# Low halves one or two units behind the high halves in the attentions of a two-block transformer kernel

## The chip, the core and the metric

The kernel runs on one core of a Trainium2 chip. The metric is device time in microseconds of one execution, as the median of several runs. The profile is of one further execution of the same program.

## The reference

Two transformer parts run one after the other, all in float32, on 512 tokens (the "latent" side) of width 1024; the first part also carries 256 context tokens.

- First part, two layers. A modulated RMS norm, one projection to queries (8 heads of 64), keys and values (2 groups of 64), and two gated inputs. Queries and keys get an RMS norm and a rotary embedding. `s = einsum('bkgqd,bkmd->bkgqm', q, k)`, `p = softmax(s)`, `einsum('bkgqm,bkmd->bkgqd', p, v)`; the latent queries see context and latent keys (768), the context queries (first layer only) the 256 context keys. Beside it a spatial gating block (4 groups). Their results are put together and multiplied by `w_out`; then a squared-ReLU feed-forward.
- Second part, two layers. A gated feed-forward, a mixer, another gated feed-forward. The mixer has 6 MLA heads (96 wide), a pooling branch and 6 "Fox" heads (64 wide, with a cumulated decay added to the scores), both attentions causal over 512 keys.

So there are five attention stretches: context and latent in layer 1, latent in layer 2, and the two mixers.

## The kernel before

**High and low halves.** A matrix product is made in a reduced format: each float32 operand x is split into a high half, ScalarE's copy of x to that format, and a low half, x minus high, which VectorE makes (`low`, L1844 and L1845: a subtraction with two tensor operands). TensorE adds high x high and the cross products (L819 to L821 for the weights' products). Weights are split the same way, by `split` on ScalarE (L1398) and on VectorE (L1779), one chunk of 128 output columns at a time in two buffers. SP's queue loads a chunk when the low half of the chunk two before is made.

**The order.** The code of each engine is one long list written out by hand; engines meet through counting semaphores, and each engine works in order. So an instruction that waits holds up all that stands behind it on its engine.

**An attention** is a loop over units; a unit is one head and 128 queries. Two heads make a pair, and their units alternate, so a pair has 8 units (4 in the context attention). Units: 16 context, 32 latent, 48 mixer. In step u:

- TensorE (`scores`, L1304 and L1305, or L1319 to L1322 in the mixer) makes the scores of unit u in one of 2 slots (4 in the mixer), as soon as the exponential of the unit that had the slot is through. It waits for the low halves of a head's queries (`q_los`) only at the head's first unit, and for those of the keys (`k_los`). Then `turn_p` (L1338) transposes the weights of unit u-3 (u-4 in the mixer), and `values` (L1366) multiplies two units' weights with the values.
- VectorE takes the negated maximum (L2269), in the first part multiplied by the query's scale (L2274), then the reciprocal of the sum of unit u-1 (L2280) and, in the first part, copies the second group of turned weights (L2287).
- ScalarE copies turned weights (L1720), then makes the exponential with its sum (L1730), which waits for VectorE's maximum.
- GpSimd multiplies the weights of a unit by the reciprocal (L2366), and in the mixer sets constant rows for heads to come (L2373 to L2376).

**Work for later that lies between.** At given units ScalarE makes high halves and VectorE the low ones: of the queries of the next pair's heads (`prepares`: units 1 and 3 of a pair, 0 and 2 in the context attention; in the mixer both queries and keys, `prepare2`, and for four Fox heads a third, small piece), of a finished pair's result (`take_out` on ScalarE, `lower_out` on VectorE), of the gated block's results (`gm`: high at odd units from 3, low at the even unit behind), of the pooling branch (high at 6, low at 7), and of the first two weight chunks of the product to come (ScalarE at 2 and 3, VectorE at 3 and 4). Queries' and results' low halves stand at the same unit as the high halves. `lower_k` makes both low halves of the second key group at unit 2, in the context attention of layer 1 and in the latent attention of layer 2.

One load of the modulation weights on SP's queue also waits for the last query low of the context attention.

The loop of VectorE around the change:

Of the kernel before, what the change touches and what calls it, by code (L numbers as in the profile page):

```python
# [23 lines left out]
KD = D // P  # L24
# [77 lines left out]
def build_program(nc, a, out):  # L102
    from contextlib import ExitStack
    ctx = ExitStack()
    with ctx:
# [151 lines left out]
        for l in range(L):  # L257
# [17 lines left out]
            for s in more[::-1]:  # L275
                nq = W[s] // P
                keys = C + T if s == "lat" else C
                U = 8 * nq
# [316 lines left out]
        def prepares(st, u):  # L595

            pair, r = divmod(u, 2 * st.nq)
            at = (1, 3) if st.nq > 2 else (0, 2)
            if r not in at:
                return None  # L600
            hd = 2 * pair + 2 + at.index(r)
            if st.first:
                if hd < st.heads:
                    return st.s, hd
                return ("lat", hd - st.heads) if st.s == "ctx" else None
            return hd if hd < st.heads else None

# [51 lines left out]
        with nc.Block() as block:  # L659
# [1104 lines left out]
            def _(dve):  # L1764
# [97 lines left out]
                def lower_k(qk, kv):  # L1862

                    own = slice(64 * kv, 64 * kv + 64)
                    dve.wait_ge(S["k_his"], qk.at("k_his", 2 * kv + 2))
                    for half in range(2):
                        low(k_lo[kv][64 * half:64 * half + 64, :], k_all[own, :], k_hi[own, kv, :]
                            ).then_inc(S["k_los"], 1)

                for st in stages:  # L1870
# [383 lines left out]
                    elif st.kind == "attention":  # L2254
# [9 lines left out]
                        for u in range(U + lag(st) + 3):  # L2264
# [23 lines left out]
                            if st.first and u >= 4 and u % 2 == 0 and u // 2 - 1 <= len(st.gm):  # L2288

                                s2, g = st.gm[u // 2 - 2]  # L2290
                                dve.wait_ge(S["gm_hi"], st.at("gm_hi", u // 2 - 1))
                                low(HL[s2][:, 4 + g, :], zt(6 + g, s2), HH[s2][:, 4 + g, :]).then_inc(S["gm_lo"], 1)
                            if not st.first and u == 7:
# [3 lines left out]
                            if u < U and prepares(st, u):  # L2297
                                if st.first:
                                    n_prep += 1
                                    prepare(st.at("q_his", n_prep), *prepares(st, u))  # L2300
                                else:
                                    n_prep += 2
                                    prepare2(st, st.at("q_his", n_prep - 1), prepares(st, u))
                            if not st.first and u in (3, 4):
                                split(st.chunk0 + u - 3, u - 3, KD)
                            if st.first and st.last_keys and u == 2:
                                lower_k(st.qk, 1)
                            v = u - lag(st) - 3
# [112 lines left out]
```

## Time and profile before

| | |
|---|---|
| median of 3 runs | 3521.12 us (3520.13 to 3521.68) |
| the profiled execution | 3524.67 us |
| its span in the trace | 3522.9 us |
| busy: TensorE / VectorE / ScalarE / GpSimd | 3410.5 / 1836.8 / 1200.4 / 369.0 us |
| chain that ended last, by engine | PE 87%, DVE 6%, ACT 4%, issue 2%, POOL 1% |
| mean granted TensorE clock | 0.982 |

PE is TensorE's products, PEld its loads of the stationary operand, DVE VectorE, ACT ScalarE, POOL GpSimd. Busy time of an engine is the time in which one of its instructions runs; the ends of matmuls are modelled, so a busy TensorE need not be at its peak. "Chain" is the work followed back from the last instruction, at each step to what released it. PEclk is the clock that TensorE was granted, as a share of 2.4 GHz; it has two levels, 1.0 and 0.5, and other values are means over a stretch. In a timeline row, the bracket gives how long the engine had been idle and what released it.

### The profile page before, as it was taken

How to read it: one execution, taken by the hardware profiler on the slowest of the kernel's cores; microseconds unless marked ns; L12 is line 12 of the kernel's file. 1: busy time of each engine (PE TensorE's matmuls, PEld its weight loads, DVE VectorE, ACT ScalarE, POOL GpSimd, SP SyncE). 2: the span in 40 equal slices, each digit the busy share in tenths (PEclk: the TensorE clock that was granted, in tenths of full speed). 3: DMA queues.
4: the chain of work that ended last, by engine and by line, in shares of the span. 5: the costliest groups of instructions: out<-in, count | busy, mean ns of one | idle time of the engine just before them, and what ended most of it. 6: DMA issues, size and time to landing. Idle time of an engine off the chain costs nothing.

```text
span 3522.9 us, 47185 instructions
## 1 busy us (share of the span) xinstructions
PE 3410.5 (97%) x17172; PEld 2804.5 (80%) x17172; DVE 1836.8 (52%) x2785; ACT 1200.4 (34%) x1886; POOL 369.0 (10%) x415
## 2 busy tenths in 40 slices
PE   9989999999998999999999989999999999899999
PEld 5867888888877788888888667888888886678887
DVE  5766866455357444454345665434543455654343
ACT  4354222122146332333232364323332323643232
POOL 0013200000202200020001132000200011320001
PEclk9989999999999999999999989999999999999999
DMA  6300343333220133333333302333333333023332
GB/s 220 118 29 25 96 137 106 117 130 125 61 72 24 49 95 96 96 95 95 97 99 102 83 25 60 97 99 95 90 101 96 95 96 83 25 61 98 98 95 90
DMA packets 551251, 314.75 MB, mean 89 GB/s; under 512 B 31102, under 2 KB 524888, under 8 KB 551128
## 3 DMA queue, kind: packets, MB, share of 16 engines
q1 hardware_dynamic: 550608, 312.99, 29.9%
q8 instruction: 76, 1.25, 0.1%
q14 instruction: 47, 0.39, 0.0%
q10 hardware_dynamic: 520, 0.13, 0.0%
HBM read 310.98 MB, written 2.10 MB: 89 GB/s over the span
## 4 chain that ended last, share of the span: by engine, by line
PE 87%; DVE 6%; ACT 4%; issue 2%; POOL 1%; DMA 0%; SPq 0%; DVEq 0%; ACTq 0%; POOLq 0%
PE ps L819 26%; PE ps L821 26%; PE ps L820 26%; PE ps L1338 2%; PE ps L1366 1%; DVE nmax L2269 1%; PE ps L974 1%; DVE scr L1956 1%; ACT scr L1730 1%; PE ps L1304 1%; ACT w_hi_sb L1398 1%; DVE hl_lat L1944 0%; PE ps L1138 0%; DVE x_ctx L1784 0%; PE ps L1244 0%
## 5 line engine op out<-in xcount | busy, mean ns | idle before, releaser
L1779 DVE TENSOR_TENSOR w_lo_sb<-w_raw,w_hi_sb 128x1024 fp32r<-128x1024 f32 (+1 forms) x460 | 588.5, 1280 | 1236.3 <-ACT w_hi_sb L1398 1234.7
L1398 ACT ACTIVATE w_hi_sb<-w_raw 128x1024 fp32r<-128x1024 f32 (+1 forms) x460 | 506.3, 1101 | 1382.2 <-PE ps L821 1351.4
L819 PE MATMUL ps<-hh_lat,w_lo_sb 128*128 128x512 f32 x1808 | 720.1, 398 | 6.0 <-DVE w_lo_sb L1779 1.9
L820 PE MATMUL ps<-hl_lat,w_hi_sb 128*128 128x512 f32 x1808 | 706.0, 391 | 0.0
L821 PE MATMUL ps<-hh_lat,w_hi_sb 128*128 128x512 f32 x1808 | 705.6, 390 | 0.0
L819 PEld LDWEIGHTS ps<-hh_lat,w_lo_sb 128*128 128x128 f32 x1808 | 341.2, 189 | 84.6 <-issue 6.7
L820 PEld LDWEIGHTS ps<-hl_lat,w_hi_sb 128*128 128x128 f32 x1808 | 340.9, 189 | 74.9 <-issue 6.3
L821 PEld LDWEIGHTS ps<-hh_lat,w_hi_sb 128*128 128x128 f32 x1808 | 340.6, 188 | 72.2
L819 PE MATMUL ps<-h2h,w_lo_sb 128*128 128x512 f32 x704 | 275.2, 391 | 1.9 <-DVE z L2240 1.5
L820 PE MATMUL ps<-h2l,w_hi_sb 128*128 128x512 f32 x704 | 274.0, 389 | 0.0
L819 PE MATMUL ps<-m2h,w_lo_sb 128*128 128x512 f32 x704 | 273.9, 389 | 0.0
L821 PE MATMUL ps<-h2h,w_hi_sb 128*128 128x512 f32 x704 | 273.9, 389 | 0.0
L821 PE MATMUL ps<-m2h,w_hi_sb 128*128 128x512 f32 x704 | 273.9, 389 | 0.0
L820 PE MATMUL ps<-m2l,w_hi_sb 128*128 128x512 f32 x704 | 273.9, 389 | 0.0
L819 PE MATMUL ps<-m1h_lat,w_lo_sb 128*128 128x512 f32 x512 | 200.4, 391 | 2.7 <-DVE x_ctx L2177 2.7
L820 PE MATMUL ps<-m1l_lat,w_hi_sb 128*128 128x512 f32 x512 | 199.5, 390 | 0.0
L821 PE MATMUL ps<-m1h_lat,w_hi_sb 128*128 128x512 f32 x512 | 199.4, 389 | 0.0
L2334 POOL TENSOR_TENSOR x_ctx<-x_lat 128x512 f32<-128x512 f32 x7 | 7.3, 1042 | 1577.8 <-DVE x_lat L2177 1577.8
L819 PEld LDWEIGHTS ps<-h2h,w_lo_sb 128*128 128x128 f32 x704 | 132.2, 188 | 31.1 <-DVE z L2240 2.3
L2366 POOL TENSOR_SCALAR scr<-scr,rinv 128x768 f32<-128x768 f32 (+4 forms) x120 | 90.3, 753 | 616.1 <-DVE rinv L2280 615.3
L820 PEld LDWEIGHTS ps<-h2l,w_hi_sb 128*128 128x128 f32 x704 | 132.2, 188 | 27.7 <-issue 0.5
L821 PEld LDWEIGHTS ps<-h2h,w_hi_sb 128*128 128x128 f32 x704 | 132.2, 188 | 27.7
(361 smaller groups left out, 5359.7 us busy)
## 6 DMA issues: line engine op xcount, KB each, us to landing
w_raw<-in_ffn_w_gu SPq DMA_DIRECT2D x176, 512.0 KB, 3.8
w_raw<-in_w_ff SPq DMA_DIRECT2D x128, 512.0 KB, 4.0
w_raw<-in_ffn_w_down SPq DMA_DIRECT2D x64, 704.0 KB, 4.5
z<-in_w_mod SPq DMA_DIRECT2D x64, 512.0 KB, 5.1
w_raw<-in_w_in SPq DMA_DIRECT2D x56, 512.0 KB, 3.8
w_raw<-in_w_out SPq DMA_DIRECT2D x32, 512.0 KB, 3.9
scr<-in_w_mod SPq DMA_DIRECT2D x16, 512.0 KB, 5.1
scr<-in_w_mod SPq DMA_DIRECT2D x2, 2048.0 KB, 14.5
```

Source lines behind the costliest of these rows:

```text
L819: nc.tensor.matmul(dst, wl, hi[:, k, 0:n], start=(k == 0), stop=False)
L820: nc.tensor.matmul(dst, wh, lo[:, k, 0:n], start=False, stop=False)
L821: mm = nc.tensor.matmul(dst, wh, hi[:, k, 0:n], start=False, stop=(k == kt - 1))
L974: mm = nc.tensor.matmul(bank(5 + n % 3)[0:2, :], silu_c[:, :, k], mod_slot(n)[:, k, :], start=(k == 0), stop=(k == KD - 1))
L1304: nc.tensor.matmul(dst[:, c0:c1], q, k_hi[:, hd // 4, c0:c1], start=True, stop=False)
L1338: mm = nc.tensor.transpose(bank(4 + i % 2)[:, j * P:(j + 1) * P], p[:, kt * P:(kt + 1) * P], ident)
L1366: mm = nc.tensor.matmul(pair_bank(st, pair)[64 * r:64 * r + 64, qt * P:(qt + 1) * P], val, att_pt(st, v - 1 + r, kt * P, (kt + 1) * P), st ...
L1398: nc.scalar.activation(w_hi_sb[:, slot, 0:width], w_raw[:, slot, 0:width], ACT.Copy).then_inc(S["w_hi"], 1)
L1730: nc.scalar.activation(att_p(st, u, n), s_slot(st, u, n), ACT.Exp, bias=nmax[:, i:i + 1], scale=q_scale(st, u) if st.first else 1.0, accum ...
L1779: nc.vector.tensor_tensor(w_lo_sb[:, slot, 0:width], w_raw[:, slot, 0:width], w_hi_sb[:, slot, 0:width].bitcast(F32), ALU.subtract).then_i ...
L1956: nc.vector.scalar_tensor_tensor(norm_tmp[i % 2][:, 0:W[s]], X[s][:, m, :], st.a_col(s, m), rs_home(st, s), ALU.mult, ALU.mult).then_inc(S ...
L2366: nc.gpsimd.tensor_scalar(pr, pr, rinv[:, i:i + 1], 0.0, ALU.mult, ALU.add).then_inc(S["p_norm"], 1)
```

## The change

The order of VectorE's instructions inside the attention loops changes; no instruction is added, and no other engine's list changes.

- The low halves of queries (and keys in the mixer) come two units behind the high ones in the latent and mixer attentions, one unit behind in the context attention (`low_behind`).
- The low half of a pair's result comes later by as many units.
- The low halves of the gated block's results go from even to odd units, two units behind the high ones.
- In the mixer the pooling low halves go from unit 7 to 8, and the low halves of the two weight chunks from units 3 and 4 to 5 and 6.
- The second key group's two low halves go from unit 2 to units 4 and 6, one each.

```diff
@@ -604,6 +604,10 @@
+
+        def low_behind(st):
+
+            return 2 if st.nq > 2 else 1
@@ -1859,11 +1863,11 @@
-                def lower_k(qk, kv):
+                def lower_k(qk, kv, halves=(0, 1)):

                     own = slice(64 * kv, 64 * kv + 64)
                     dve.wait_ge(S["k_his"], qk.at("k_his", 2 * kv + 2))
-                    for half in range(2):
+                    for half in halves:
                         low(k_lo[kv][64 * half:64 * half + 64, :], k_all[own, :], k_hi[own, kv, :]
                             ).then_inc(S["k_los"], 1)
@@ -2285,27 +2289,28 @@
-                            if st.first and u >= 4 and u % 2 == 0 and u // 2 - 1 <= len(st.gm):
+                            if st.first and u >= 5 and u % 2 and u // 2 - 1 <= len(st.gm):
...
-                            if not st.first and u == 7:
+                            if not st.first and u == 8:
...
-                            if u < U and prepares(st, u):
+                            w = u - low_behind(st)
+                            if 0 <= w < U and prepares(st, w):
                                 if st.first:
                                     n_prep += 1
-                                    prepare(st.at("q_his", n_prep), *prepares(st, u))
+                                    prepare(st.at("q_his", n_prep), *prepares(st, w))
                                 else:
                                     n_prep += 2
-                                    prepare2(st, st.at("q_his", n_prep - 1), prepares(st, u))
-                            if not st.first and u in (3, 4):
-                                split(st.chunk0 + u - 3, u - 3, KD)
-                            if st.first and st.last_keys and u == 2:
-                                lower_k(st.qk, 1)
-                            v = u - lag(st) - 3
+                                    prepare2(st, st.at("q_his", n_prep - 1), prepares(st, w))
+                            if not st.first and u in (5, 6):
+                                split(st.chunk0 + u - 5, u - 5, KD)
+                            if st.first and st.last_keys and u in (4, 6):
+                                lower_k(st.qk, 1, (u // 2 - 2,))
+                            v = u - lag(st) - 3 - low_behind(st)
                             if 0 <= v < U - 1 and pair_ends(st, v):
                                 lower_out(v // (2 * st.nq))
```

## Rows read from the trace of the kernel before

**Rows 1.** Windows; columns: us, PE, PEld, DVE, ACT, POOL busy, PEclk, DMA, GB/s.

```profile
205.00:236.00 31.00, 19.04 (x116) 13.60 (x118) 19.88 (x71) 19.08 (x54) 7.72 (x16) 0.72 0.06 15
236.00:330.00 94.00, 83.32 (x730) 67.90 (x727) 64.26 (x152) 59.86 (x116) 29.11 (x32) 0.95 0.04 13
1076.00:1172.00 96.00, 84.41 (x728) 68.87 (x729) 66.61 (x154) 60.69 (x115) 29.91 (x32) 0.93 0.02 7
2048.00:2138.00 90.00, 77.28 (x571) 62.16 (x570) 53.08 (x134) 62.70 (x179) 38.30 (x66) 0.87 0.05 13
3016.00:3106.00 90.00, 73.23 (x567) 58.30 (x567) 52.77 (x134) 62.70 (x178) 38.28 (x66) 0.92 0.05 13
```

**Rows 2.** Waits, 236 to 330 us: total us, times, longest us.

```profile
ACT scr L1730 <- DVE nmax L2274: 20.3, 22, 2.4
DVE q_hl L1845 <- ACT q_hl L1423: 10.1, 6, 2.1
...
DVE hl_lat L1845 <- ACT hh_lat L1423: 6.7, 4, 3.0
```

**Rows 3.** Timeline, first latent attention: start us, us, engine, operation, idle before.

```profile
248.89 0.69 DVE L1845 TENSOR_TENSOR q_hl<-z,q_hl 64x512 fp32r<-64x512 f32 x1 [2.15 <-ACT q_hl L1423]
```

**Rows 4.** Timeline, first latent attention, two units with TensorE full.

```profile
254.13 1.53 PE L1366 MATMUL ps<-scr 128*64 128x128 f32 x24
...
258.06 0.95 DVE L2269 TENSOR_REDUCE nmax<-ps 128x1 f32<-128x768 f32 x1
...
258.57 1.53 PE L1366 MATMUL ps<-scr 128*64 128x128 f32 x24
...
259.37 0.91 POOL L2366 TENSOR_SCALAR scr<-scr,rinv 128x768 f32<-128x768 f32 x1 [0.55 <-DVE rinv L2280]
259.51 1.30 DVE L1845 TENSOR_TENSOR hl_lat<-z,hh_lat 128x512 fp32r<-128x512 f32 x1
```

**Rows 5.** Windows, latent attentions by eights of exponentials (303.43: seven).

```profile
259.76:282.78 23.02, 19.51 (x178) 15.20 (x174) 17.75 (x40) 15.74 (x33) 7.06 (x9) 1.00 0.01 1
282.78:303.43 20.65, 18.68 (x174) 15.10 (x172) 15.32 (x38) 14.63 (x29) 7.09 (x8) 1.00 0.01 2
303.43:320.19 16.76, 16.00 (x160) 13.50 (x154) 10.91 (x31) 11.48 (x22) 6.38 (x7) 1.00 0.00 1
1082.55:1105.04 22.49, 17.10 (x110) 13.25 (x112) 17.62 (x37) 14.30 (x28) 7.54 (x8) 0.77 0.00 1
```

**Rows 6.** Instructions of L1845, low halves: ns min/median/max, first and last start.

```profile
L1845 DVE TENSOR_TENSOR hl_lat<-ps,hh_lat x20: 691/692/693, 276.8 to 3104.3; 128x512 fp32r<-128x512 f32 x20
```

**Rows 7.** Timeline, second latent attention, VectorE, unit 2.

```profile
1087.37 2.54 DVE L1845 TENSOR_TENSOR k_lo<-scr,k_hi 64x768 fp32r<-64x768 f32 x2
```

**Rows 8.** Windows, context attention: units 0 to 7, units 8 to 14.

```profile
206.64:219.64 13.00, 8.34 (x42) 6.66 (x42) 9.36 (x31) 7.82 (x25) 3.38 (x7) 0.52 0.00 1
219.64:233.56 13.92, 7.76 (x66) 5.27 (x62) 8.79 (x32) 8.33 (x24) 3.38 (x7) 0.97 0.00 1
```

**Rows 9.** Windows, second mixer: units 1 to 4, 17 to 24, 33 to 40.

```profile
3019.06:3028.83 9.77, 5.15 (x27) 4.03 (x26) 6.93 (x16) 6.45 (x17) 2.61 (x4) 0.79 0.07 19
...
3046.92:3062.03 15.11, 11.36 (x93) 8.73 (x92) 9.81 (x24) 11.04 (x33) 9.53 (x16) 1.00 0.00 1
...
3077.12:3089.84 12.72, 10.88 (x92) 8.72 (x92) 7.60 (x22) 9.78 (x30) 5.51 (x10) 1.00 0.00 1
```

**Rows 10.** Timeline, first mixer, a unit that prepares a Fox head.

```profile
2079.17 0.39 ACT L1730 ACTIVATE z<-ps,nmax 128x128 f32<-128x128 f32 x1
...
2079.51 1.84 ACT L1423 ACTIVATE split_x<-z 64x512 fp32r<-64x512 f32 x3
...
2080.18 1.73 DVE L1845 TENSOR_TENSOR split_x<-z,split_x 64x512 fp32r<-64x512 f32 x2 [1.06 <-ACT split_x L1423]
...
2081.93 0.75 DVE L1845 TENSOR_TENSOR split_x<-z,fox_cr 6x512 fp32r<-6x512 f32 x1
...
2083.17 0.47 ACT L1730 ACTIVATE z<-ps,nmax 128x256 f32<-128x256 f32 x1 [1.20 <-DVE nmax L2269]
```

## The prediction

> **What bounds the kernel now.** I read the page first (TensorE busy nearly all the span), then the chain of waits, which puts 87% of the span on TensorE. So only stretches where TensorE runs dry can give time back. The change touches the five attention stretches alone; the windows over them [rows 1] add up to 401.0 us with TensorE busy 337.3. The rest, 31.00 - 19.04 = 12.0 us in the context attention and 10.7, 11.6, 12.7 and 16.8 us in the other four, is 63.7 us and the ceiling of what filling gaps can bring. No engine is full there: VectorE 256.6 us, ScalarE 265.0. The gaps come from order, not load.
>
> The waits of the first latent attention [rows 2] name the order. VectorE stands 10.1 us in six waits for ScalarE's high halves of queries and 6.7 us in four for those of results; ScalarE stands 20.3 us for VectorE's scaled maximum. The timeline of one such unit [rows 3]: VectorE idles 2.15 us until the high half is there and only then makes the low half and goes on to the next maximum. All the while the scores of that unit had been ready: VectorE's queue holds the maximum behind a low half that nobody needs for units to come.
>
> Without such a wait the loop is TensorE's: from one value product to the next [rows 4] it takes 258.57 - 254.13 = 4.44 us for two units, so 17.8 us for eight. The last eight units, which prepare nothing, run close to that: 16.76 us for seven, 0.76 of it idle [rows 5]. The eight units from 259.76 take 23.02 us and the next eight 20.65 [rows 5], with 3.5 and 2.0 us of TensorE idle. That is the cost that the change aims at.
>
> **Part 1: low halves of queries, results and block inputs later, latent attentions.** Nothing is added; the order on VectorE alone changes. Each moved low half finds its high half made a unit or two ago, so the waits of [rows 2] go: 10.1 + 6.7 us of VectorE's time in this stretch, of which TensorE's idle time is the part that reaches the end. Next late is VectorE itself. Its unit costs 259.51 - 258.06 = 1.45 us [rows 4], and a low half of a block input 1.30. A fed eight (four block lows, two query lows at 0.69 [rows 3], one result low at 0.69 [rows 6]) is then 11.6 + 5.2 + 1.4 + 0.7 = 18.9 us, against TensorE's 17.8: VectorE is just the bound where the block inputs are lowered, and not elsewhere (at most 14.9). So the eight of 23.02 falls to about 18.9 but loses no more than the idle 3.5 in TensorE's count; I take 2.9 of it, 1.6 of the 2.0 in the next (block lows in its first half), 0.5 of the last 0.76, and 1.3 in the first eight: 6.3 us. Ends: 3 (one gap in two refilled by the odd units, which now carry two lows) and 9.
>
> The second latent attention has half the block lows, but its first eight take 22.49 us with 5.4 idle [rows 5]. There the two lows of the second key group stand together for 2.54 us [rows 7] at unit 2, ahead of a maximum. In two pieces at units 4 and 6 they are some 1.3 us each when TensorE has scores in stock; the maximum of unit 3 comes these 2.5 us earlier, and the wait for the first query high, of the kind of [rows 3], goes as well. I take 3.3 of the 5.4, and 3.4 of the 6.2 idle elsewhere in that stretch, in all 6.7 us of 11.6. Ends 3 and 11. The keys' deadline is head 4, unit 16 here and unit 8 in the context attention; the pieces are done at 4 and 6, so the wait on them moves only there, by under 1 us.
>
> **Part 2: context attention.** 13.00 us for its first eight units, 13.92 for the next seven [rows 8], the latter at nearly full clock with 6.2 idle. VectorE is busy 8.79 of 13.92. Here lows are one unit behind; the wait for a high half is then about the high itself, beside an exponential. TensorE is no bound in the second half. VectorE's 8.79 and ScalarE's 8.33 busy us are the floor for seven units, 5.1 us below the 13.92; I take 4.0 us of that and 1.0 of the first, where the key lows are only spread and the clock is low (0.52). Sum 5.0; ends 2 and 8.
>
> **Part 3: the two mixer attentions.** 9.77 us for units 1 to 4 with 4.6 idle, then 15.11 us for the eights with Fox heads and 12.72 for the next [rows 9]. A unit that prepares a head [rows 10]: three highs 1.84 us, lows from 2080.18 to 2082.68 (1.73 and 0.75), the next exponential 4.00 us after the last. The same again two units on. So before, each stop is the first high plus the lows, some 3.3 us beyond a plain unit, 6.6 for both heads. Afterwards the first highs stand alone (1.8), the first head's lows lie beside the second head's highs (1.8 more on ScalarE, or 2.5 on VectorE less one exponential), and the second head's lows stand alone (2.5 less the 1 us that ScalarE still has to do): 5.1 to 5.6. That is a gain of only 1 to 1.5 an eight, 1.3 taken; two such eights. The result's low saves about 1 us of VectorE's wait per pair, where TensorE isn't dry for lack of it: 1.0 for the eight of 12.72, 0.3 in the last. The first units lose their wait before the weight split, which moves to units 5 and 6 and there holds a maximum 1.2 us each while TensorE has work: I take 1.5 (first mixer, which has 12.7 us idle to the second's 16.8) and 2.6 us (second) out of idle. Sum 5.4 + 6.5 = 11.9; ends 0 (three lumps as dear as two) and 20.
>
> **Part 4: queues.** The weight loads two chunks on wait for the splits, now some three units later; they are needed after the attention, tens of us away: nothing. The modulation block's load behind the last context query low moves by under one unit, with the whole latent attention as cover: nothing. If that cover were gone each would cost its delay, 1 to 5 us.
>
> **Part 5: the shared access.** What spoke against the old order also shielded it. After its wait a query low met an idle GpSimd and took 0.69 us [rows 3]. A block low that follows the reciprocal at once took 1.30 [rows 4], while GpSimd normalized from 259.37 for 0.91; the same subtraction with one operand in PSUM takes 0.69 [rows 6]. So lows that come right behind the reciprocal may cost 0.6 more, or hold GpSimd's normalization by their own length. For the 6 + 6 query lows of the latent attentions and 20 heads of mixer lows most fall where VectorE has slack. I charge 2 us in all; ends 0 and 37 (see the slower rival). The Trainium skill (SBUF — State Buffer, section "SBUF: two separate sides") states this rule: a VectorE operation with two SBUF inputs and a GpSimd operation that reads SBUF exclude each other for a whole instruction. The trace agrees, 1.30 against 0.69 us.
>
> **Sum.** 6.3 + 6.7 + 5.0 + 11.9 - 2 = 27.9 us. The profiled execution took 3524.67 us (its span is 3522.9), so 3496.8; the median of the runs is 3.55 us below it: 3493.
>
> **The clock.** It is at 1.2 GHz for part of each stretch (granted 0.72 to 0.95 [rows 1]; 0.77 in the first eight of the second latent attention, after 5.4 us of idle in them [rows 5]). Fewer gaps may keep it at 2.4 GHz. Five stretches x (1 - granted) x 2 is about 78 us at the lower level; even a quarter of that regained, at half a us each, is 10 us. It is not in the sum.
>
> **Rivals.**
> - *The lumps stay* (0.22). Lows that lay beside highs now stand alone, and odd units carry block and query lows together. Mixers give 0, the latent attentions 4 each, the context 4: 12 us, 3509. For it: VectorE 18.9 against 17.8 in fed eights, three lumps for two. Against: four scores in stock in the mixers, TensorE well below full there [rows 9].
> - *The clock comes too* (0.11): 27.9 + 10 to 15, 3481 at 10, 3478 and below at the end. For it: the clock rows. Against: entry into each attention is unchanged, and that is where it falls.
> - *No change* (0.03): TensorE's idle time just moves from one unit to another, so that it catches up and starves again; its busy 16.00 of 16.76 [rows 5] shows that it sets the pace where it has work. Within 3 us.
> - *Slower* (0.03): in place of the wait on ScalarE each of some 60 lows (8 + 6 + 6 + 40) excludes GpSimd or is excluded, 0.61 us each on VectorE or on the transposes' path: 37 us lost against 28 gained, 3530. It decides from 0.5 us per low on the path. Against: TensorE takes up a normalized tile units later, and existing block lows pay it in a loop that still keeps TensorE full [rows 4].
> - That the lows aren't released at all cannot be: their waits are on counts that ScalarE reached a unit or more before.
>
> **Numbers.** The forecast, 20 to 36 us gained (3485 to 3501), has 0.61. To hold 8 in 10 the range reaches to the lumps' 3509 and to the clock's 3479. Faster by over 0.2% (7 us, about what a measurement of this kernel can tell from no change): all of forecast, clock and lumps, 0.94; same 0.03; slower 0.03.
>
> **What would show it.** Right: VectorE's waits on ScalarE's high halves near zero in the five stretches (only short ones in the context attention); eights of the latent attentions at 18 to 19 us; mixer eights at about 13.7 instead of 15.1; TensorE idle in the five stretches near 35 us instead of 64; the other stages unchanged. Wrong: new waits of the transposes on GpSimd, ScalarE waiting as long for maxima as before (20.3 us in the first latent attention), low halves of 1.3 us throughout, or scores waiting for low queries or keys.

## The result: faster, by more than the range allowed

| | before | after |
|---|---|---|
| median of the runs taken side by side | 3521.40 us (4 runs, 3520.13 to 3524.96) | 3479.13 us (4 runs, 3476.11 to 3479.71) |
| after / before | | 0.9877 (0.986 to 0.9894) |
| span of the profiled execution | 3522.9 us | 3477.7 us |
| mean granted TensorE clock | 0.982 | 0.985 |

The change takes 42.3 us off the median (27.9 were forecast) and 45.2 off the profiled span. The ratio is the record's, from all the single runs; the medians as they stand give 0.9880. Applied to the median that the prediction started from it gives 0.9877 x 3521.12 = 3477.8 us (3478.9 with 0.9880), just under the lower end of 3479. The sign and the mechanism came as forecast, the size did not.

The page of the changed kernel: busy times, and the chain by engine. VectorE's and ScalarE's work is what it was; GpSimd is busy 18.1 us longer with the same 415 instructions; TensorE's share of the chain rises from 87 to 90%.

```profile
PE 3396.5 (98%) x17172; PEld 2800.6 (81%) x17172; DVE 1838.3 (53%) x2785; ACT 1200.7 (35%) x1886; POOL 387.1 (11%) x415
...
PE 90%; DVE 5%; ACT 3%; issue 1%; POOL 1%; DMA 0%; SPq 0%; DVEq 0%; ACTq 0%; POOLq 0%
```

The windows of [rows 1] in the changed kernel, each over the same work:

```profile
205.00:229.50 24.50, 19.84 (x127) 13.94 (x128) 20.23 (x71) 18.76 (x54) 9.88 (x16) 0.78 0.07 16
229.50:312.80 83.30, 78.79 (x721) 66.25 (x718) 65.33 (x150) 60.26 (x116) 29.18 (x32) 0.97 0.05 16
1058.40:1146.60 88.20, 81.77 (x728) 68.64 (x728) 68.98 (x153) 61.01 (x115) 29.17 (x32) 0.94 0.03 7
2019.40:2102.20 82.80, 75.07 (x571) 61.87 (x570) 52.20 (x134) 62.67 (x179) 46.63 (x66) 0.88 0.05 14
2978.50:3060.50 82.00, 74.27 (x567) 61.29 (x566) 52.28 (x134) 62.74 (x180) 46.65 (x66) 0.88 0.05 14
```

They add up to 360.8 us against 401.0. TensorE is idle in 31.1 us of them (360.8 - 329.7); 35 was forecast from 63.7. But its busy time fell too, from 337.3 to 329.7, for the same products (2712 and 2714 matmuls in the windows). That is what no term of the sum had.

Narrower windows sort it by attention: context with first latent, second latent, first mixer, second mixer. First before, then after:

```profile
206.64:320.19 113.55, 92.06 (x738) 73.00 (x738) 80.02 (x209) 73.96 (x162) 35.02 (x46) 0.89 0.05 15
1082.55:1162.42 79.87, 70.23 (x606) 57.10 (x606) 58.03 (x137) 54.85 (x104) 28.09 (x30) 0.94 0.00 1
2050.93:2130.89 79.96, 69.37 (x509) 55.95 (x508) 50.09 (x127) 59.22 (x171) 36.90 (x64) 0.85 0.05 14
3018.61:3099.35 80.74, 66.09 (x509) 52.78 (x508) 50.10 (x127) 59.42 (x171) 36.89 (x64) 0.92 0.05 14
```

```profile
206.77:302.95 96.18, 87.90 (x739) 71.39 (x739) 80.32 (x208) 73.99 (x162) 37.24 (x46) 0.92 0.06 18
1064.87:1137.01 72.14, 67.41 (x607) 56.81 (x607) 59.86 (x136) 55.37 (x104) 27.35 (x30) 0.95 0.01 1
2022.28:2095.06 72.78, 66.31 (x498) 55.00 (x497) 48.71 (x126) 59.26 (x171) 45.55 (x65) 0.86 0.06 16
2981.47:3054.25 72.78, 66.31 (x498) 55.01 (x497) 48.70 (x126) 59.26 (x172) 45.58 (x65) 0.86 0.06 16
```

| less, in us | forecast | time | TensorE idle | TensorE busy |
|---|---|---|---|---|
| context + first latent | 5.0 + 6.3 = 11.3 | 17.4 | 13.2 | 4.2 |
| second latent | 6.7 | 7.7 | 4.9 | 2.8 |
| first mixer | 5.4 | 7.2 | 4.1 | 3.1 |
| second mixer | 6.5 | 8.0 | 8.2 | -0.2 |
| all four | 29.9 | 40.2 | 30.4 | 9.8 |

The time of a stretch is firmer than its split. These windows run from the first exponential to the last, and the mixers' now hold 498 matmuls against 509: 11 fall behind the last exponential. The wide windows above, with as many matmuls, give 32.7 us to idle and 7.5 to busy time. And the clock differs from trace to trace: in the last experiment, the same kernel once more, the four stretches took 312.1 us with TensorE busy 284.7 (313.9 and 287.9 here), and in the two kernels that leave some of them alone the untouched ones took 353.3 with 300.9 busy (354.1 and 297.8 here). So the time falls by 39.4 to 42.0 us, of which, in these windows, 25 to 30 are idle time and 10 to 16 busy time.

The rest of the span is 5.0 us shorter (45.2 - 40.2). Run again in the last experiment, the same kernel doesn't show that: the stretch between the first two attentions took 762.36 us before, 761.92 after and 765.08 in the repeat, the next one 888.51, 885.27 and 888.28. In all fourteen traces of the record the span outside the five attentions is between 3163.5 and 3171.1 us, whatever the order in them (3168.8 before, 3163.8 after). So this part is chance, and only about 40 us belong to the change.

The stretches that answer to [rows 5, 8, 9], in the changed kernel: context units 0 to 7 and 8 to 14; first latent attention, the same two eights and last seven; second latent, first eight; first mixer, units 1 to 4, 5 to 15, 16 to 23, 32 to 39, counted from 0 (the last two are what [rows 9] calls 17 to 24 and 33 to 40).

```profile
206.77:217.62 10.85, 8.84 (x45) 6.50 (x46) 9.43 (x33) 7.71 (x25) 4.08 (x7) 0.63 0.00 1
217.62:226.34 8.72, 7.44 (x62) 4.93 (x60) 8.20 (x32) 8.07 (x25) 4.69 (x8) 1.00 0.01 2
249.93:269.23 19.30, 18.86 (x179) 15.82 (x179) 18.05 (x41) 15.83 (x31) 7.30 (x8) 1.00 0.01 2
269.23:287.24 18.01, 17.58 (x175) 14.90 (x173) 16.09 (x39) 14.72 (x28) 7.28 (x8) 1.00 0.01 2
287.24:302.95 15.71, 15.15 (x149) 12.93 (x145) 10.31 (x30) 11.60 (x22) 6.37 (x7) 1.00 0.00 1
1064.87:1085.03 20.16, 16.60 (x114) 13.36 (x115) 18.03 (x36) 14.29 (x28) 6.39 (x7) 0.84 0.00 1
2022.72:2028.83 6.11, 3.49 (x23) 3.02 (x22) 3.36 (x11) 6.11 (x18) 2.60 (x4) 0.87 0.00 0
2028.83:2047.86 19.03, 18.86 (x119) 15.39 (x118) 13.76 (x34) 14.05 (x42) 12.35 (x11) 0.68 0.20 56
2047.86:2061.19 13.33, 11.24 (x99) 9.03 (x100) 9.39 (x24) 10.96 (x33) 9.70 (x16) 1.00 0.01 1
2074.51:2086.22 11.71, 11.71 (x98) 9.98 (x94) 7.76 (x22) 9.92 (x30) 7.30 (x10) 0.85 0.01 1
```

The waits of the first latent attention, as in [rows 2] (229 to 313 us): VectorE's 10.1 us for query high halves are gone, ScalarE's wait for the maximum is halved from 20.3 to 10.5, and VectorE now waits for scores. The 3.0 us for a result's high half are the last pair's, behind which nothing is left to do.

```profile
ACT scr L1734 <- DVE nmax L2278: 10.5, 17, 2.4
DVE nmax L2273 <- PE ps L1309: 9.6, 12, 1.4
...
DVE hl_lat L1849 <- ACT hh_lat L1427: 3.0, 1, 3.0
```

### The profile page after: what moved, and what is told of

The parts are those of the page before. It is cut to its first block, busy times and chain, and to the rows that moved or that the text cites. A ratio compares the mean times of both kernels' runs of the same rounds, so it can differ in the third digit from the quotient of the medians.

```text
span 3477.7 us, 47185 instructions
## 1 busy us (share of the span) xinstructions
PE 3396.5 (98%) x17172; PEld 2800.6 (81%) x17172; DVE 1838.3 (53%) x2785; ACT 1200.7 (35%) x1886; POOL 387.1 (11%) x415
## 4 chain that ended last, share of the span: by engine, by line
PE 90%; DVE 5%; ACT 3%; issue 1%; POOL 1%; DMA 0%; SPq 0%; DVEq 0%; ACTq 0%; POOLq 0%
PE ps L823 26%; PE ps L824 26%; PE ps L825 26%; PE ps L1370 2%; PE ps L1342 2%; PE ps L978 1%; PE ps L1308 1%; DVE scr L1960 1%; ACT w_hi_sb L1402 1%; DVE nmax L2273 1%; PE ps L1309 1%; DVE hl_lat L1948 0%; PE ps L1142 0%; DVE x_ctx L1788 0%; PE ps L1248 0%
## 5 line engine op out<-in xcount | busy, mean ns | idle before, releaser
L2371 POOL TENSOR_SCALAR scr<-scr,rinv 128x768 f32<-128x768 f32 (+4 forms) x120 | 97.8, 815 | 574.6 <-DVE rinv L2284 574.1
L823 PEld LDWEIGHTS ps<-m2h,w_lo_sb 128*128 128x128 f32 x704 | 132.1, 188 | 27.5
```

Of the source, the lines that this page charges most:

```text
L823: nc.tensor.matmul(dst, wl, hi[:, k, 0:n], start=(k == 0), stop=False)
L2371: nc.gpsimd.tensor_scalar(pr, pr, rinv[:, i:i + 1], 0.0, ALU.mult, ALU.add).then_inc(S["p_norm"], 1)
```

## The experiments

All diffs are against the changed kernel (its lines stand 4 above those of before). "After" is 3479.13 us, 0.9877.

### Which half of the change, and which kind of low half

Only the attentions of the first parts, or only the mixers, keep the new order:

```diff
 # first parts only
-            return 2 if st.nq > 2 else 1
+            return (2 if st.nq > 2 else 1) if st.first else 0
 # (pooling lows and weight splits back at units 7, 3 and 4)
 # mixers only
+            return 0 if st.first else 2
 # (block lows at even units, key lows together at unit 2)
```

> The new order in the context and the two latent attentions alone, the mixers as before. Order theory (each stretch gives back its own idle time): the trace of the changed kernel gives 7.4 + 0.4 us in the context attention, 9.6 in the first latent and 7.7 in the second, so some 25 us less than before, 3496. Clock-chance theory (part of the 42 us comes from the level the clock happens to have elsewhere): the three stretches give the same 25, but the stretches outside the attentions move by several us, up or down, without an instruction of theirs changed.

> The new order in the two mixers alone. Order theory: 7.2 and 8.0 us in the mixers, so some 15 us less than before, 3506, and with the run before this one adds up to about 40 of the 42. If the two together give clearly less than 42, the parts help each other through the clock or through what follows them; if the mixers give nothing (the rival of the three lumps), 3521.

Measured: first parts only 3499.25 us, 0.9932 (0.9915 to 0.9948), 25.5 us less than before; mixers only 3506.46 us, 0.995 (0.9933 to 0.9967), 18.3 less (both against 3524.76). The sum, 43.8, is the whole change's 42.3 within the spread: the two halves don't help or disturb each other. The untouched attentions kept their time within 0.8 us (79.96 and 79.94 us for the mixers in the first, against 79.96 and 80.74 before; 113.48 and 79.89 for the others in the second, against 113.55 and 79.87).

Then by kind: only queries' and keys' lows behind, or only results' lows.

```diff
 # queries and keys only
-                            v = u - lag(st) - 3 - low_behind(st)
+                            v = u - lag(st) - 3
 # results only
-            return 2 if st.nq > 2 else 1
+            return 0
...
+                            v = u - lag(st) - 3 - (2 if st.nq > 2 else 1)
 # (in both: block, pooling and second key lows and splits as before)
```

> Of the changed kernel only the low halves of queries (in the mixers queries and keys) stand two units behind (one in the context attention); results', gated block's, pooling, weights' and second keys' low halves stand where they stood before. If the query waits carry the gain in proportion to the waits in the trace of before (10.1 us of 19.4 in the first latent attention, 15 of 23 in a mixer): 55 to 65% of the 42 us, 3495 to 3498. If the parts hide one another (one wait left per pair is enough to hold the loop): under 15 us less than before.

> Only the results' low halves behind by two units (one in the context attention), all others as before. In proportion to the waits: 25 to 35% of the gain, 3507 to 3511. In the context attention its four results' lows cost a pair of units 1.9 us instead of two units' 1.4, so 1.5 to 2 us there; 1.0 for each of five pairs of a mixer where TensorE is short of work.

Measured: queries only 3492.73 us, 0.9912 (0.9895 to 0.9928), 33 less than 3525.80; results only 3507.84, 0.9954 (0.9938 to 0.9971), 18 less. Together 51, more than the whole, and queries alone gave more than the 55 to 65% expected of them (78%). One reading is that a stall of one kind that goes leaves room in which part of the other would have hidden. The eight of 23.02 us bears it out: it took 19.68 with queries alone and 21.97 with results alone, 4.4 us less in sum, but 19.25 with both (the block lows still at even units, in the last of the four kernels below), 3.8 less. The other moves of the change (block, pooling and key lows, weight splits), which neither kernel has, may cost something on the whole; that would show the same way and was not tried.

### Is it the order, or the clock that comes with it?

The mixer's start holds the largest piece at the lower clock. The timeline of the changed kernel's first mixer: a head's high halves and then a weight chunk's occupy ScalarE for 1.14 and 1.05 us, the copy (L1724) that a transpose needs comes behind them, and TensorE has stood for 2.62 us. After this the clock is at 1.2 GHz for most of units 5 to 15 (0.68 granted), with 0.17 us idle in 19.

```profile
2025.97 1.14 ACT L1427 ACTIVATE split_s<-scr 96x512 fp32r<-96x512 f32 x2
...
2027.01 1.05 ACT L1402 ACTIVATE w_hi_sb<-w_raw 128x1024 fp32r<-128x1024 f32 x1
2027.96 0.26 ACT L1724 ACTIVATE scr<-ps 128x128 f32<-128x128 f32 x1
...
2028.36 0.66 PE L1342 MATMUL ps<-konst,z 128*128 128x128 f32 x2 [2.62 <-ACT scr L1724]
```

Two kernels: one with both halves of the two weight chunks split near the attention's end, one that keeps them but gives TensorE four products of 128x512 more in each of units 2 to 5, into a bank that nobody reads.

```diff
 # late split
-                            if not st.first and u in (2, 3):
-                                split(st.chunk0 + u - 2, u - 2, KD)
+                            if not st.first and u in (41, 42):
+                                split(st.chunk0 + u - 41, u - 41, KD)
...
-                            if not st.first and u in (5, 6):
-                                split(st.chunk0 + u - 5, u - 5, KD)
+                            if not st.first and u in (43, 44):
+                                split(st.chunk0 + u - 43, u - 43, KD)
 # filler, behind the scores of a unit
+                                if not st.first and 2 <= u < 6:
+                                    for i in range(4):
+                                        nc.tensor.matmul(bank(7), hh_lat[:, 0, 0:P], hh_lat[:, 0, :], start=True, stop=True)
```

> The changed kernel, with the high and low halves of the first two weight chunks moved from the mixer's units 2, 3 and 5, 6 to units 41, 42 and 43, 44, where no head is prepared. In the trace of the changed kernel TensorE stands 2.62 us at the start of each mixer for a copy by ScalarE that lies behind a weight high half of 1.05 us. If that is the next limit: both halves leave, 1.5 to 2.5 us less per mixer, and the clock's fall to 1.2 GHz right after that gap should go or shrink (12 us at the lower level, worth up to 6 more per mixer). Together 3 to 15 us less than the changed kernel. If the clock falls whatever the gap is: 3 to 5 us less.

> The changed kernel, with four products of 512 columns into a bank that is free then, behind the scores of units 2 to 5 of each mixer: 16 products, 3.4 us of TensorE's time at full clock, that compute nothing used. If the clock falls because TensorE stands at the mixer's start: it stays at 2.4 GHz through units 5 to 15 (12 us at the lower level now), those units take 19.0 - 6 us, and the mixer loses at most 3.4 for the products: 0 to 5 us less per mixer, 0 to 10 in all. If what TensorE does has no bearing on the clock there: 12 us at the lower level as before and up to 3.4 us more per mixer, 3 to 7 us slower.

Windows of the first mixer with the late split: units 1 to 4, 5 to 15, the whole attention.

```profile
2024.93:2029.49 4.56, 4.56 (x23) 4.27 (x22) 3.36 (x11) 4.33 (x15) 2.58 (x4) 0.63 0.00 0
2029.49:2045.42 15.93, 13.88 (x123) 11.46 (x123) 10.89 (x32) 13.38 (x42) 9.62 (x11) 1.00 0.00 1
2024.48:2093.92 69.44, 62.84 (x498) 51.45 (x497) 47.88 (x126) 58.32 (x172) 44.52 (x65) 0.93 0.05 13
```

The same with the filler (units 1 to 4, 5 to 15), then units 5 to 15 of the changed kernel's repeat:

```profile
2029.05:2035.16 6.11, 6.11 (x34) 5.26 (x33) 3.50 (x11) 6.11 (x18) 2.58 (x4) 1.00 0.00 0
2035.16:2054.00 18.84, 17.09 (x123) 14.07 (x121) 13.77 (x34) 14.17 (x41) 12.32 (x11) 0.82 0.19 57
```

```profile
2033.02:2051.93 18.91, 17.30 (x118) 14.27 (x116) 13.75 (x34) 14.03 (x41) 12.32 (x11) 0.73 0.19 56
```

Late split: 3475.32 us, 0.9863 (0.9846 to 0.9879); this mixer takes 69.44 instead of 72.78. Filler: 3482.04, 0.9884 (0.9867 to 0.99); the mixer 71.93. The filler's products run where TensorE stood (same 6.11 us) and hold its clock at 2.4 GHz there. In units 5 to 15 that takes 1.8 us off TensorE's busy time (18.86 to 17.09) but puts 1.6 us of idle time in its place: the clock alone is worth 0.2 us there, since another engine is as late. The repeat says the same without a filler: 1.6 us less busy, 18.91 us in all.

The whole mixer took 71.93 us with the filler, 0.9 less than the changed kernel's 72.78, but that is not the filler's: two kernels with the same mixer order and no filler ("mixers only", and "block lows even" below) took 71.93 and 71.91. In the second mixer units 5 to 15 took 17.53 us with the filler at 0.90 of the clock, and 17.67 and 17.66 in these two kernels at 0.74.

The late split, which also takes the splits out of those units, gets 3.1 in them and 1.9 to 3.4 in a mixer (69.44 and 69.41 against 71.36 to 72.78 for the changed order in all traces). It doesn't end the low clock, though: units 1 to 4 now have 0.63 granted. Neither kernel gave the 6 us a mixer expected of a clock that sets the time. In a mixer a faster TensorE pays only where the other engines' order lets it. In device time both kernels are within the interval of the changed one; the windows carry the reading.

### Two units behind, or one, and where in the step

A mixer's eight with Fox heads fell only from 15.1 to 13.3 us. VectorE's rows of that eight in the changed kernel, then ScalarE's; the bracket is the wait before:

```profile
2051.89 0.16 DVE L2284 RECIPROCAL rinv<-rsum 128x1 f32<-128x1 f32 x1 [1.45 <-ACT z L1734]
2051.97 1.27 DVE L1849 TENSOR_TENSOR split_x<-z,split_x 64x512 fp32r<-64x512 f32 x2
...
...
2055.77 0.69 DVE L1849 TENSOR_TENSOR split_s<-z,split_s 64x512 fp32r<-64x512 f32 x1
```

```profile
2052.82 1.80 ACT L1427 ACTIVATE split_s<-z 64x512 fp32r<-64x512 f32 x3
...
2058.73 0.69 ACT L1734 ACTIVATE z<-ps,nmax 128x512 f32<-128x512 f32 x1 [2.18 <-DVE nmax L2273]
```

The first head's low halves could begin at 2050.44, when the last maximum is done. They stand behind a reciprocal, and this one waits 1.45 us for an exponential that ScalarE runs only after its own high halves. Later the second head's lows stand alone, and ScalarE waits 2.18 us for the maximum behind them. Four kernels vary this: everything one unit behind; queries' and keys' lows ahead of the step's wait and reciprocal; in the mixers behind the wait, but ahead of the reciprocal (this one separates the wait from the reciprocal, and so from GpSimd's normalization, which the reciprocal releases); and the changed kernel with only the block lows back at even units.

```diff
 # one unit
-            return 2 if st.nq > 2 else 1
+            return 1
 # one unit, and also gm_even alone
-                            if st.first and u >= 5 and u % 2 and u // 2 - 1 <= len(st.gm):
+                            if st.first and u >= 4 and u % 2 == 0 and u // 2 - 1 <= len(st.gm):
 # ahead: these lines moved up, before the wait for p_exp and the reciprocal
+                            w = u - low_behind(st)
+                            if 0 <= w < U and prepares(st, w):
+                                if st.first:
+                                    n_prep += 1
+                                    prepare(st.at("q_his", n_prep), *prepares(st, w))
+                                else:
+                                    n_prep += 2
+                                    prepare2(st, st.at("q_his", n_prep - 1), prepares(st, w))
 # exp first: the mixers' part of them between that wait and the reciprocal
```

> The changed kernel with all low halves one unit behind instead of two (the gated block's at even units, one behind, as before the change). If it is enough that the high half has been made by the time VectorE comes to it: the step's reciprocal already waits for the exponential ahead of that high half, so one unit leaves a wait of about one high half (0.6 us) and less in the mixers; within 5 us of the changed kernel, 3479 to 3485. If the distance matters: half of the gain, 3495 to 3505.

> The changed kernel with the low halves of queries and keys ahead of the reciprocal of their step instead of behind it. Shared-access theory: behind the reciprocal each low meets GpSimd's normalization (a normalization of 3.23 us beside lows at the first mixer's unit 5 in the changed kernel's trace); ahead of it they don't, GpSimd's busy time falls by 10 us or more, and if that was on the path the kernel gains 2 to 8 us. If GpSimd's blocked time is off the path, as TensorE takes a unit's weights three or four units later: no gain, and the later reciprocal costs at most 3 us: 3479 to 3482.

> The changed kernel, in the mixers with the low halves of queries and keys ahead of the step's reciprocal but behind its wait for the exponential. It parts two explanations of the 1.5 us an eight that the mixers gained in the run with the low halves ahead of both. If the gain was that GpSimd's normalization no longer runs beside the low halves: it stays, eights with Fox heads 11.8 us, 3474 or below. If it was that VectorE no longer stands until the exponential behind ScalarE's high halves is through (1.45 us idle ahead of the reciprocal in the changed kernel): it goes, eights at 13.3 us, 3479 to 3482.

> The changed kernel with the gated block's low halves at even units as before, one unit behind, and the queries' two behind at odd units. If the second eight of the first latent attention (19.30 us against 18.22 in the one-unit version) is slow because odd units carry two low halves: it falls to about 18.2 and the kernel gains 1 to 2 us. If it is the query low halves' distance: it stays at 19.3. Either way in the noise of the total; the trace decides.

| | us | ratio | latent eight | Fox eight | next eight |
|---|---|---|---|---|---|
| after | 3479.13 | 0.9877 (0.986 to 0.9894) | 19.30 | 13.33 | 11.71 |
| one unit | 3467.60 | 0.9839 (0.9822 to 0.9855) | 18.22 | 12.38 | 10.17 |
| ahead | 3474.62 | 0.9857 (0.984 to 0.9873) | 19.91 | 11.84 | 9.86 |
| exp first | 3478.18 | 0.9872 (0.9856 to 0.9887) | (order as after) | 13.00 | 10.90 |
| block lows even | 3477.00 | 0.9873 (0.9856 to 0.989) | 19.25 | (order as after) | (order as after) |

Only "one unit" is clear of the changed kernel in device time, and it missed both of its expectations (3479 to 3485, or 3495 to 3505) by being faster. The span outside the attentions differs by up to 7.6 us between traces, so the sums over the attentions tell more:

| us | first parts (context + two latent) | two mixers | all |
|---|---|---|---|
| after / its repeat | 168.3 / 166.7 | 145.6 / 145.4 | 313.9 / 312.1 |
| one unit | 165.5 | 134.4 | 299.9 |
| ahead | 171.8 | 131.0 | 302.8 |
| exp first | 166.8 | 143.3 | 310.0 |
| block lows even | 166.6 | 143.3 | 309.8 |

So most of what one unit gives is in the mixers too (11.2 of 14.0 us). The windows behind the table before: one unit (latent eight, Fox eight, next), then ahead (the same three).

```profile
248.70:266.92 18.22, 17.90 (x177) 15.25 (x174) 17.54 (x40) 15.76 (x32) 7.03 (x9) 1.00 0.01 2
...
2048.01:2060.39 12.38, 10.81 (x99) 8.92 (x100) 10.04 (x24) 10.85 (x33) 10.29 (x16) 1.00 0.00 0
2072.79:2082.96 10.17, 10.17 (x98) 8.59 (x96) 7.95 (x22) 9.62 (x31) 6.40 (x10) 1.00 0.01 2
```

```profile
250.28:270.19 19.91, 18.83 (x180) 15.77 (x179) 18.24 (x41) 16.05 (x32) 7.30 (x8) 1.00 0.01 2
2054.88:2066.72 11.84, 11.04 (x99) 8.94 (x100) 9.65 (x24) 10.88 (x32) 10.37 (x16) 1.00 0.00 0
2078.48:2088.34 9.86, 9.86 (x94) 8.30 (x88) 8.01 (x22) 9.69 (x30) 5.93 (x10) 1.00 0.01 2
```

The place in the step counts most in the mixers. Ahead of the wait an eight is 1.5 us shorter; behind the wait but ahead of the reciprocal only 0.3. The next eight compares badly with the 11.71 us, which had 0.85 of the clock: at full clock the changed order takes 11.03 or 11.04 there (mixers only, filler, block lows even), exp first 10.90, one unit 10.17, ahead 9.86. So nearly all of it is the wait, and little what the reciprocal releases. The run "ahead" by itself had both signs expected of the shared access: GpSimd 11.4 us less busy and 4.5 us gained. Exp first takes 16.5 us off GpSimd's busy time (387.1 to 370.6) without the gain. (It isn't a clean exchange: with the reciprocal later, TensorE's transposes wait 2.8 us for GpSimd in two Fox eights, 0.2 in the changed kernel.) In the trace of "ahead" the low halves start with the maximum's end and ScalarE's wait of 2.18 us is 0.43:

```profile
2057.40 1.54 DVE L1849 TENSOR_TENSOR split_x<-z,split_x 64x512 fp32r<-64x512 f32 x2
...
2064.27 0.69 ACT L1734 ACTIVATE z<-ps,nmax 128x512 f32<-128x512 f32 x1 [0.43 <-DVE nmax L2273]
```

In the latent attentions it is the other way: ahead costs 0.6 us (19.91), one unit gains 1.1 (18.22), and that isn't the parity of the block lows (19.25 with these alone). One unit is enough for a query's high half to be there, and it puts the query's low on another unit than the block's. That the second half of this is the cause was not tried by itself. Nor were one unit behind and the place ahead of the wait tried together in a mixer.

### The version made of these

First parts one unit behind with block lows at even units; mixers two behind and ahead; late split:

```diff
-            return 2 if st.nq > 2 else 1
+            return 1 if st.first else 2
 # (late split, mixers' lows ahead, block lows at even units, as above)
```

> What the runs so far point to together: context and latent attentions with all low halves one unit behind and the gated block's at even units; mixers with low halves two units behind, ahead of the reciprocal and its wait; results' low halves as far behind; the first two weight chunks' halves at the mixer's units 41, 42 and 43, 44. Sum of the pieces in the traces: 3.3 us in the first-part attentions and 3.6 us per mixer for the reciprocal's place, and for the weights' halves 2 to 3 per mixer: 14 to 17 us less than the changed kernel, 3462 to 3465, if they add; if the clock takes some back, as low as it was for the one-unit version, 3468. Below 3460 would mean that the clock stays at 2.4 GHz through the start of the mixers as well.

> The changed kernel itself once more, to see in a second trace what of the 45 us between the two profiled executions is the program's and what the clock's phase. Order theory alone: the same stretches to 0.1 us. Clock's share: stretches without an instruction of the change (the product stages between the attentions) took 4.9 us less in the changed kernel's trace, with 12 us less at 1.2 GHz; if that is chance, a second trace shows other amounts at 1.2 GHz there (30 to 45 us) and 3 to 6 us more time; if it belongs to the program, 30 us again.

Measured: 3457.51 us (5 runs), 0.9813 (0.98 to 0.9827): some 66 us under before (3523.39) and 21.6 under the change, below the 3462 to 3465 expected. The attentions fell by 26.4 us: 3.5 in the first parts and 11.3 and 11.5 in the mixers, where late split (3.3) and ahead (7.3) alone make 10.6. The clock stays at 2.4 GHz through units 5 to 15, as a time below 3460 was to mean, but not in units 1 to 4 (0.59). The changed kernel again gave 3479.52, 0.9869 (0.9854 to 0.9884), so the distance isn't the chip's. Units 5 to 15 and the whole of the first mixer (72.78 in the changed kernel):

```profile
2027.80:2041.97 14.17, 13.76 (x122) 11.43 (x120) 10.68 (x31) 13.37 (x42) 6.97 (x11) 1.00 0.00 1
...
2023.14:2084.58 61.44, 59.03 (x498) 49.09 (x497) 49.40 (x126) 57.70 (x172) 40.84 (x65) 0.97 0.05 15
```

## Why the prediction was right, and where it failed

- **What bounds the kernel.** Right that only the gaps' stretches give; wrong that their 63.7 us of idle time are "the ceiling of what filling gaps can bring". TensorE's busy time isn't all work. In the two eights of the first latent attention [rows 5] the clock is 1.00 before and after, and busy fell from 38.19 to 36.44 us with as many products; in the two eights behind the first of the second latent attention, also at 1.00, from 37.14 to 35.65. In the first pair 1.5 of the 1.75 us are transposes. There are 96 of them, each as long as before (columns behind the bar: us busy, mean ns; first before, 259.76 to 303.43, then after, 249.93 to 287.24):

```profile
L1338 PE MATMUL ps<-konst,scr 128*128 128x128 f32 x96 | 15.1, 278 | 3.9 <-DVE scr L2287 3.7
```

```profile
L1342 PE MATMUL ps<-konst,scr 128*128 128x128 f32 x96 | 13.6, 275 | 0.2 <-DVE scr L2291 0.2
```

  96 x 278 ns is 26.7 us, so their spans overlap. With 3.9 us of stops between them they overlap less and cover 1.5 us more: time that counts as busy and is not work.
- **Part 1, latent.** The idle terms were good: 2.9 and 1.6 us taken, 3.1 and 1.5 measured in the two eights. The fed eight was put at 18.9 and took 19.30. But it "loses no more than the idle 3.5" failed: it lost 3.7, 0.65 of it busy time; the three windows lost 7.4 us against 5.0 taken (the last of them holds 149 matmuls against 160, so its 0.85 us less of busy time may be those). In the second latent attention the first eight gave 2.3 instead of 3.3, the rest 5.4 instead of 3.4.
- **Part 2, context.** 5.0 forecast, 2.15 + 5.20 = 7.35 measured. The second half took 8.72 us, at the floor of 8.79 busy us named there, of which only 4.0 of 5.1 had been taken. Three other traces with this order have 9.86 or 9.87 there, so one of these us comes and goes.
- **Part 3, mixers.** 11.9 forecast, 15.2 measured. The lump arithmetic held where it was made: the Fox eight was put at 13.8 and took 13.33, the next at 11.7 and took 11.71 (11.03 at full clock). What was short is the start: the second mixer's units 1 to 4 went from 9.77 to 6.10 us (2981.92 to 2988.02), 3.7 less against 2.6 taken. In the first mixer units 5 to 15 got longer (before, then after at 19.03 above, where 2.62 us of standing came ahead; 15.93 with the weight splits taken out of them, so the splits that the change moved there have a share in it):

```profile
2061.15:2078.46 17.31, 17.31 (x124) 14.30 (x124) 10.94 (x31) 13.81 (x41) 6.13 (x11) 0.77 0.17 49
```

- **Part 4, queues.** No stage outside the attentions got longer beyond what the traces differ by, as forecast.
- **Part 5, shared access.** The exclusion is there and nearly off the path; the 2 us charged for it were too many. TensorE's transposes waited 2.6 and 4.0 us for GpSimd in the two mixers before and wait 0.2 in each now, and "exp first" brings GpSimd back to 370.6 us busy (369.0 before the change) for a total that is the same within the interval. At 2029.07 GpSimd's normalization of 128x384 takes 3.23 us beside two low halves and a weight split on VectorE that follow each other without a gap, where one of the same shape takes 0.59 at 2058.86. Of GpSimd's 18.1 us of added busy time 17.3 stand in the mixers (36.90 to 45.55 and 36.89 to 45.58), and with the old order in them alone they are back at 36.72 and 36.73. The Trainium skill (SBUF — State Buffer, section "SBUF: two separate sides") has VectorE operations with two SBUF inputs and GpSimd operations that read SBUF exclude each other; the trace agrees, 3.23 against 0.59 us. Here three such VectorE operations follow each other (0.67, 0.68 and 1.21 us, from 2028.89 to 2031.30), and the 3.23 us run from 2029.07 to 2032.30.

```profile
2029.07 3.23 POOL L2371 TENSOR_SCALAR z<-z,rinv 128x384 f32<-128x384 f32 x1 [1.90 <-DVE rinv L2284]
...
2058.86 0.59 POOL L2371 TENSOR_SCALAR scr<-scr,rinv 128x384 f32<-128x384 f32 x1 [1.42 <-DVE rinv L2284]
```

- **The clock and the ceiling: the step that failed.** The sum held TensorE's busy time fixed. "It is not in the sum" was said of a clock term that the same paragraph put at 10 us, and the stalls that count as busy were not seen. The idle terms were 29.9 us and the trace shows 30.4. TensorE's busy time fell by 9.8 in the attentions, and the sum had nothing for it. With the 2 us charged in Part 5 that makes 12.3 of the 14.4 us between forecast and result; 2 us are within the runs' spread. Of the busy time the granted clocks tie about 4 us to the clock: the time at 1.2 GHz is the sum of 2 x (1 - granted) x us, 71.5 us before and 63.4 after, at half a us each (78.0 and 65.9 in the wide windows, about 6). This is an estimate: clocks rounded to 0.01 leave some 2 us, and it takes TensorE as busy all the while at the lower clock. It isn't even: the second mixer had more time at 1.2 GHz than before (20.4 us against 12.9), and no less busy time. The four eights at full clock hold 3.2 us (1.75 + 1.49) that are not the clock. The two together, 7 to 9 us, are the size of what fell in this pair of traces (7.5 to 9.8); how it divides is good to some 2 us at best.
- **The rivals.** "The clock comes too" (0.11) had the size right, in part by luck: the clock gives some 4 to 6 of the 10 to 15 us that it named. The filler shows the limit of its mechanism, since a clock that is kept up gave 0.2 us where another engine was next. "The lumps stay" fell, though lumps do stay: in two Fox eights ScalarE's longest wait for a maximum is 2.2 us with two units, 1.1 with one, and 0.43 in the row above with the lows ahead. "Slower" fell: the exclusion costs GpSimd its 18 us, and little of it is on the path.

## What to carry to other kernels

When an engine's in-order list holds a step that waits for another engine, ask for the least distance at which its input is there, and put it ahead of the next wait in the list, not behind: one unit instead of two was worth 11.5 us more here, and in the mixers the place before the wait 1.5 us an eight. Try the place stretch by stretch: in the latent attentions the same move cost 0.6 to 1.4 us in four of the eights. Forecast a filled gap by its idle time and by what TensorE's own busy time gives back (lower clock, short stalls that count as busy): here a third on top. Then check which engine is next before crediting the clock.

## What the runs showed of the hardware that was not expected

- A stand of 2.62 us ahead of units 5 to 15 of a mixer is followed by a granted clock of 0.68 through 19 us in which TensorE is idle 0.17 us, in both mixers. In the repeat TensorE was at 0.72 already in units 1 to 4, stood 1.35 us at this place and had 0.73 in units 5 to 15. With the weight splits moved away, which removes the stand, these have 1.00, and units 1 to 4 have 0.63; with products in its place and the splits kept it is 1.00 first and 0.82 after. The first mixer's units 5 to 15 took 18.84 to 19.03 us in all of these but the one with the splits moved.
- TensorE's busy time is no floor. The same 96 transposes, 278 and 275 ns each at full clock, cover 15.1 us when stops lie between them and 13.6 us when they don't.
- The same kernel profiled twice differed by 3.2 and 3.0 us in two product stages in which the change touches nothing (761.92 and 765.08, 885.27 and 888.28), more than several of the parts that were told apart. Windows over the changed stretch tell such parts better than the total.
